# Splitting the first two mixers' projections and output products into high and low halves

## What is computed

```
# even mixer: 4 retention heads of 128, 8 stick-breaking heads of 64
h = x @ w_in_even                       # 1024 x 3584
y = concat(silu(rg) * norm(retention(rotary(rq), rotary(rk), rv)),
           stick_breaking(sq, sk, sv))
x = layer_norm(ALPHA * x + y @ w_out_even); x = layer_norm(ALPHA * x + conv_ffn(x))
# odd mixer: 8 differential heads of 2 x 64
q, k, v = split(x @ w_in_odd)           # 1024 x 3072
p = softmax(q k^T / 8 + rel_bias)       # two per head, causal
o = (p[0] - lam * p[1]) @ v;  o = rms(o) * sub_g * (1 - lam_init)
x = layer_norm(ALPHA * x + o @ w_out_odd); x = layer_norm(ALPHA * x + conv_ffn(x))
```

## Time and profile before

| | us |
|---|---|
| median of 3 runs | 2521.33 (2520.19 to 2523.63) |
| the profiled execution | 2520.85 |
| its span, first to last instruction | 2519.2 |
| PE busy in the span | 2223.6 (88%) |
| DVE, ACT, POOL busy | 1326.6, 1000.7, 332.1 |
| TensorE clock granted, mean | 0.934 |

### The profile page before, as it was taken

The page is one execution under the profiler, slowest core; times in us unless marked ns, Lnnn a source line. Parts: engine busy times, 40 slices in busy tenths (PEclk is TensorE's granted clock), DMA queues, the critical chain, the costliest instruction groups (busy, mean ns, idle before and its releaser), DMA issues. The chain is left out here.

```text
span 2519.2 us, 27351 instructions
## 1 busy us (share of the span) xinstructions
PE 2223.6 (88%) x9734; PEld 1639.5 (65%) x9734; DVE 1326.6 (53%) x1786; ACT 1000.7 (40%) x1100; POOL 332.1 (13%) x299
## 2 busy tenths in 40 slices
PE   8989988999997889799999986757792999999994
PEld 4446647888885555448888875646452788777773
DVE  1221025555442333426554445997613898888885
ACT  1114323343321333303343323123311787777783
POOL 1000000000000000000000001757201122222221
PEclk9989999999998999899999997878885999999997
DMA  9011205743225210204332223211014999999995
GB/s 279 26 43 67 67 17 192 242 117 100 101 67 146 57 50 18 67 0 130 89 108 84 101 67 73 67 50 34 17 37 150 346 398 399 399 398 400 397 399 212
DMA packets 283158, 378.58 MB, mean 150 GB/s; under 512 B 13385, under 2 KB 181501, under 8 KB 282937
## 3 DMA queue, kind: packets, MB, share of 16 engines
q1 hardware_dynamic: 266216, 317.24, 37.6%
q0 software_dynamic: 16848, 60.09, 6.4%
HBM read 341.08 MB, written 38.84 MB: 151 GB/s over the span
## 5 line engine op out<-in xcount | busy, mean ns | idle before, releaser
L845 PE MATMUL PS<-XS,split 128*128 128x512 f32 (+1 forms) x2304 | 486.2, 374 | 13.0 <-DVE split L157 9.9
L845 PEld LDWEIGHTS PS<-XS,split 128*128 128x128 f32 x2304 | 410.4, 191 | 88.6 <-issue 10.3
L157 DVE TENSOR_TENSOR moe_split<-moe_raw,moe_split 128x2048 fp32r<-128x2048 f32 x174 | 397.8, 2288 | 87.1 <-ACT moe_split L152 86.8
L152 ACT CAST moe_split<-moe_raw 128x2048 fp32r<-128x2048 f32 x174 | 332.6, 1913 | 72.2 <-DMA moe_raw<-in_expert_w_gate 37.8
L2285 PE MATMUL PS<-moe_split,moe_x 128*128 128x512 f32 x1392 | 347.7, 400 | 8.6 <-DVE moe_split L157 4.8
L2285 PEld LDWEIGHTS PS<-moe_split,moe_x 128*128 128x128 f32 x1392 | 258.6, 190 | 72.6 <-DVE moe_x L157 13.9
L157 DVE TENSOR_TENSOR split<-ring,split 128x2048 fp32r<-128x2048 f32 x68 | 155.7, 2292 | 220.0 <-ACT split L152 220.0
L878 PE MATMUL PS<-split,XS 128*128 128x512 f32 x960 | 218.4, 389 | 0.3 <-DVE XS L157 0.3
L152 ACT CAST split<-ring 128x2048 fp32r<-128x2048 f32 x78 | 148.1, 1903 | 154.5 <-PE PS L878 110.8
L878 PEld LDWEIGHTS PS<-split,XS 128*128 128x128 f32 x960 | 180.1, 188 | 38.4 <-issue 1.1
L614 PE MATMUL PS<-ring,W 128*128 128x512 f32 x384 | 170.3, 603 | 2.9 <-issue 0.8
(11 more groups left out here) (338 smaller groups left out, 2496.3 us busy)
## 6 DMA issues: line engine op xcount, KB each, us to landing
moe_raw<-in_expert_w_gate SPq DMA_DIRECT2D x58, 1024.0 KB, 13.8
moe_raw<-in_expert_w_up SPq DMA_DIRECT2D x58, 1024.0 KB, 13.9
moe_raw<-in_expert_w_down SPq DMA_DIRECT2D x58, 1024.0 KB, 13.4
ring<-in_w_up SPq DMA_DIRECT2D x88, 512.0 KB, 5.2
ring<-in_w_down SPq DMA_DIRECT2D x44, 512.0 KB, 4.3
expert_rows<-rows POOLq DMA_DIRECT2D x4, 4096.0 KB, 30.4
expert_rows<-W POOLq DMA_DIRECT2D x29, 512.0 KB, 7.0
ring<-in_w_in_even SPq DMA_DIRECT2D x56, 256.0 KB, 5.2
```

Source lines behind the costliest of these rows:

```text
L152: act.copy(hi, raw).then_inc(sem, 1)
L157: return dve.tensor_tensor(lo, raw, hi.bitcast(F32), ALU.subtract)
L845: mm = pe.matmul(PS[:, b + q, rows], w[:, c, q, :], x_half(k, high)[:, c, rows], start=(c == 0 and m == 0), stop=(c == KC - 1 and m == 2))
```

## The change

All projections of both mixers and both output products become three products of halves. The weights come in "pieces" of 128x2048, 18 in the even block and 16 in the odd block, through the 4 raw slots and the 3 slots of `split`. q and k of a head (or pair) are one piece; v comes for two heads (or pairs) at once, in matmuls of 256 columns, and one turn of PE makes half of the tokens.

```diff
+def piece_high(k, act, n):
+    slab = k.pieces[n]
+    slab_ready(k, act, slab)
+    if n >= SPLIT:
+        act.wait_ge(k.piece_used, n - SPLIT + 1)
+    split_high(k, act, k.ring[:, slab[0], :], k.split[:, piece_slot(k, n), 1, :], k.piece_highs)
+def piece_low(k, dve, n):
+    slab = k.pieces[n]
+    dve.wait_ge(k.piece_highs, n + 1)
+    ...
+    split_low(dve, ...).then_inc(k.freed[slab[0]], 1)
```

`entry` copies high halves on ACT and adds low halves on DVE, and splits pieces 0 and 1 behind them. In retention, ACT and DVE split two more pieces per head:

```diff
@@ retention_stage, scalar
         for h in range(H):
             for part in range(2):
                 ...
                 act.copy([qT, kT][part], PS[:, part, :]).then_inc(qk_out, 1)
+            piece_high(k, act, 2 * h + 4)
...
             if h + 1 < H:
                 keep(h + 1, 2)
                 keep(h + 1, 3)
+                piece_high(k, act, 2 * h + 5)
             act.wait_ge(y_turned, h + 1)
             act.copy(YT[:, h, :], PS[:, 2, :]).then_inc(y_out, 1)
```

The stick stage makes four turns ahead (q, k and both halves of v of two pairs), then 3, 3, 2 and 0 turns within the pairs, each of which waits for the keep of the turn two before it; DVE halves the first seven chunks of y while the last pair is on its way (`halve_y`). The output stage multiplies piece 0 for all four tiles and then pieces 1 to 3 tile by tile, and `tail.early` now stands one tile earlier on ACT:

```diff
+        for t in range(NT):
+            mm = product(0, t)
+        mm.then_inc(k.piece_used, 1)
+        for t in range(NT):
+            for i in range(1, 4):
+                ...
+                mm = product(i, t)
...
+            if t == NT - 2 and tail.early:
+                tail.early.scalar(act)
```

The tail of the first feed-forward now writes halves too, and during it ACT and POOL split the first odd piece. In the differential stage POOL makes all low halves but the last, and loads the bias, which has two buffers now:

```diff
@@ diff_stage
+    def lows(pool, h):
+        for u in after[h]:
+            if u in follows and follows[u] < len(k.pieces) - 1:
+                piece_low(k, pool, follows[u])
     def gpsimd(pool):
         ...
+        for h in range(HD):
+            if h > 1:
+                pool.wait_ge(biased, 4 * (h - 2) + 4)
+            src = ...
+            pool.dma_start(bias[:, h % 2, :], src).then_inc(bias_in, 16)
+            if h > 1:
+                pool.wait_ge(bias_in, 16 * (h + 1))
+            if h == 1:
+                for n in (1, 2, 3, 4):
+                    piece_low(k, pool, n)
+                lows(pool, 0)
+            if h > 0:
+                lows(pool, h)
+        pool.wait_ge(early_high, 1)
+        split_low(pool, YT[:, 0:EARLY, :], ...).then_inc(early_low, 1)     # EARLY = 6
@@ scalar, keep(u), behind the copy
+            if u in follows and follows[u] < len(k.pieces) - 1:
+                piece_high(k, act, follows[u])
@@ vector
-        dve.wait_ge(bias_in, 16 * HD)
         for h in range(HD):
+            dve.wait_ge(bias_in, 16 * max(h + 1, 2))
             if h > 0:
                 mix(h - 1, 3)
```

More of the change, by code:

```diff
@@ L419, in sync @@
         w = A["w_in_even"][0]
[L420 to L423, removed]
-    def tensor(pe):
[L426 to L437, removed]
+        for n in (QK0, V01, QK1, V23, QK2, QK3):
+            if n in (V01, V23):
+                load_slab(k, sp, k.pieces[n], [columns(w, 3072 + 256 * (n == V23), 256)])
+            else:
+                p = (QK0, QK1, QK2, QK3).index(n)
+                load_slab(k, sp, k.pieces[n], [columns(w, 2048 + p * P + 512 * part, P) for part in range(2)])
@@ L438, in project @@
+    def tensor(pe):
+        def project(u):
+            n, what, which = turns[u]
+            if u >= 2:
+                pe.wait_ge(kept, u - 1)
+            elif u == 0:
                 pe.wait_ge(k.ret_kept, 16)
                 pe.wait_ge(k.ret_rotated, 16)
[L440 to L448, removed]
@@ L449, in project @@
-            if part == 2:
-                for t in range(NT):
-                    for c in range(KC):
[L452 to L457, removed]
+            bank = 6 + u % 2
@@ L482, in tensor @@
                 mm.then_inc(scored, 1)
-            if p < 3:
-                for part in range(3):
-                    project(p + 1, part)
+            for u in after[p]:
+                project(u)
             for hh in range(2):
@@ L647, in norm_tail @@
     k.rows_used = (normed, NT)
-    split = name in ("even", "odd", "ffn1")
+    split = name != "out2"
     xt_high = k.sem(name + "_xt_high")
@@ L651, in norm_tail @@
     st = k.stat
-    pair = (lambda t: 2 * (t % 2)) if name != "ffn0" and name != "ffn1" else (lambda t: 2 * t)
+    pair = (lambda t: 2 * t) if split else (lambda t: 2 * (t % 2))
+    turn_pair = (0, 0, 4, 6) if name in ("even", "odd") else (0, 2, 4, 6) if split else (4, 4, 4, 4)
     src = (lambda t: X[:, t, :]) if mode == "ln" else (lambda t: hrow[:, t % nh, :])
@@ L816, in early_scalar @@
         act.sem_inc(split_used, AHEAD)
-        high_w(act, 0, 0)
-        act.wait_ge(mixer_tail.product, NT)
-        high_w(act, 1, 0)
+        for i in range(2):
+            act.wait_ge(k.piece_used, len(k.pieces) - 2 + i)
+            high_w(act, i, 0)
     def early_vector(dve):
@@ L850, in tensor @@
     def tensor(pe):
+        pe.drain().then_inc(k.piece_used, 1)
         for turn in range(2):
@@ L1118, in project @@
                 for c in range(KC):
-                    mm = pe.matmul(PS[:, bank, :], view[c // 4][:, c % 4, part, :], k.XT[:, c, :],
-                                   start=(c == 0), stop=(c == KC - 1))
-            else:
-                for t in range(NT):
+                    for m, (w, high) in enumerate(((wh, 1), (wh, 0), (wl, 1))):
+                        mm = pe.matmul(PS[:, bank, :], w[:, c, part], x_half(k, high)[:, c, :],
+                                       start=(c == 0 and m == 0), stop=(c == KC - 1 and m == 2))
+            else:
+                half = turns[u][3]
+                for t in (2 * half, 2 * half + 1):
@@ L1183, in tensor @@
                 value(h - 1, 3)
-            more[0]()
+            project(after[h][0])
             turn_w(h, 0)
@@ L1189, in tensor @@
             score(h, 3)
-            more[1]()
+            project(after[h][1])
             if h > 0:
@@ L1194, in tensor @@
             turn_w(h, 2)
-            more[2]()
+            project(after[h][2])
             value(h, 2)
@@ L1246, in scalar @@
             rows(h, 1)
-            more[0]()
+            keep(after[h][0])
             leave_w(h, 0)
@@ L1253, in scalar @@
             rows(h, 3)
-            more[1]()
+            keep(after[h][1])
             if h > 0:
@@ L1257, in scalar @@
             leave_w(h, 2)
-            more[2]()
+            keep(after[h][2])
+            if h == EARLY:
+                act.wait_ge(projected, len(turns))
+                act.drain()
+                act.copy(x_half(k, 1)[:, 0:EARLY, :], YT[:, 0:EARLY, :]).then_inc(early_high, 1)
         leave_w(HD - 1, 3)
```

424 lines of the change are left out of this document (288 added, 136 removed).

## The result

The changed kernel takes 2525.73 us (median of 20 runs, 2523.12 to 2533.96), the one before 2521.98 us (20 runs) beside it: a ratio of 1.0017, 95% interval 1.0010 to 1.0024. The forecast was 2510. So the change is slower by 0.17%, less than the 0.2% that the prediction called no change. The profiled execution took 2523.86 us (span 2522.3), against 2520.85 before.

What follows compares the result with a forecast made beforehand. PE, busy 88% of the span, was taken as the bound; 7 - 12.6 - 15.5 - 18.8 - 18.6 + 3.5 + 44.4 = -10.6 from 2520.85 gave 2510 us, range 2483 to 2537.

Steps and rivals of the forecast that it cites:

- Price of the products: All changed stages: 0.227 us per fp32r product of 512 columns, 0.114 per 256; PE relieved of 107.7 us together.
- Clock: Slow clock after PE's new pauses: 3 us in retention, +8 in the differential stage, about 2 after each 11 us stop.
- Waits: New PE waits: retention 8.3 us for ACT's cast; differential stage +8, +15.6, +38.1 and, in head 7, +13.9.
- the bias: Differential stage: transfer issued behind POOL's low halves, +11.3 in heads 2, 4, 6, +2.1 in 3, 5; together +38.1.
- rival 2: Differential stage: bias tile lands late beside SP's 1 MB, at 7.8 us; 2533, slower; chance 0.25.
- POOL's hold: Differential stage: POOL's low half stops DVE, +4.6 us each in heads 1, 3, 5 and +1.8 in head 0; +15.6.
- rival 1: Differential stage: POOL's low halves don't hold DVE, so 15.6 and 7.2 us go; 2487; chance 0.17.
- The k cast: Differential stage: ACT casts 1.90 us before leave_y in heads 0, 2, 4, 6; +2.0 each, +8.
- The entry: Kernel start: DVE's low halves and the first piece's cast and low half delay PE, +7 us.
- both output products: Even and odd output stages with the feed-forward's first tokens: -18.8 and -18.6 us; the even one from 79.0 to 60.2.
- the tail: End of the first feed-forward: two pairs of low halves in DVE's chain and 0.9 us behind the last turn, +3.5.
- Rival 3: Some twenty new PE pauses add slow clock, or a semaphore hop is missing; gain and loss cancel at 2521; chance 0.10.

Runs made afterwards that it cites:

- the first experiment: The changed kernel with POOL issuing head h+1's bias transfer ahead of the low halves of head h in the differential stage: 2467.67 us, ratio 0.9784.
- the quarters: The changed kernel with the bias issued ahead of the low halves and POOL's weight-piece low halves as four 512-column instructions, differential stage: 2475.08 us, ratio 0.9822.

## Why the prediction was wrong

The direction of every stage was right, the sum was not: -10.6 us against +3.0 in the profiled executions (2520.85 and 2523.86). The 13.6 us by terms (rounded), with -0.3 from the stages that came within about 1 us and -2.0 behind them:

- **Price of the products, 12.7 us.** I took 0.227 us from the feed-forward's 960 products and 0.114 from 44. In the differential stage a turn of 24 takes 5.73 us, not 5.45, and a v half 6.00. 16 turns from 7.03 to 5.73 give 20.8 instead of 25.3, v from 58.5 to 11.74 + 6 x 6.00 = 47.7 gives 10.8 instead of 14.9. In retention 16 products of 13.90 became 48 of 11.15, eight times: 22.0 instead of 23.9. In the stick stage the eight turns give 11.3 instead of 12.6 and v 5.5 instead of 7.4, and 2.2 of these 3.2 us show in the length of the stage. A price per product from long rows leaves out what each short row pays once: 24 products take 5.73 us and 48 take 11.15, which is 0.226 each and 0.3 a row. For 256 columns 48 take 6.00 and 96 take 11.74, 0.120 each and 0.26 a row, so there the price itself was low too. The row to take was the turn.
- **Clock, 12.1 us.** Forecast 3 in retention and 8 in the differential stage. Retention's busy time fell by 13.4 us, the products alone by 22.0: 8.6. The differential stage's fell by 17.1 instead of 31.6: 14.5. These two are what is left when the products are taken out, but the granted clock fell with them, from 0.97 to 0.91 and from 0.93 to 0.81, and the first experiment gave 13.1 back with the same instructions. The prediction took the price of a short stop from one turn of 8.20 us; behind the same wait of 2.21 us head 1 of the kernel before has 7.13 and heads 2 to 6 have 7.71 to 8.12. The direct test, a pause in the kernel before, gave 10.4 us for 27 us of waiting, where I had 2 per long stop. And stops of 2.6 us, for which I had 1, put scores of 2.42 at 3.8 to 4.6.
- **Waits, -8.8 us.** In retention 6.6 instead of 8.3, in the differential stage 69.5 instead of 76.6. There, by the forecast's own steps: the bias in heads 2, 4 and 6, 10.9, 11.9 and 9.8 (forecast 11.3 each); in heads 3 and 5, 3.2 and 1.6 (2.1 each); head 7, 11.7 (13.9). The bias landed 4.3, 5.2, 5.3, 5.2, 3.2 and 3.3 us after its issue, 4.4 in the mean (4.0); SP's 1 MB ran beside it as rival 2 said, but its 7.8 us did not come. POOL's hold cost 4.2 us in heads 1, 3 and 5 (4.6), so rival 1 fell. The instruction held there is not one of mix, as I had said, but the scaling behind the bias sums (L1476). The k cast cost 1.35 in three heads, not 2.0 in four: head 0 has no leave_y.
- The entry (+6.0), both output products (-18.1, -18.2) and the tail (+3.1) came within 1 us. For the odd product the prediction shows no working: the 60.2 us of the even one would have made -20.5 of 80.7.

So the steps that failed are two terms of the sum. The price of a product was taken at 0.227 and 0.114 us where the turns measured 0.239 and 0.125. The clock was taken at 3 and 8 us where 8.6 and 14.5 came out. Together they are 24.8 us short, covered in part by waits counted too high. A difference of 10.6 between terms of over 90 us each way can't carry a sign at that accuracy. Rival 3, at a chance of 0.10, named one of the two, the clock, and no price. That its 2521 is nearly the total is luck: the waits counted too high stood against the price.

## What to carry to other kernels

Take the price of a product from a row as long as the one that will run, and put beside each new wait of PE its share for the clock: here 0.3 to 0.4 of it for stops of 7 to 12 us, half and more for stops of 2 us. That is an average, and no closer than some 10 us for a whole stage: the quarters raised busy time by 14.8 us while the waits fell. When an engine issues transfers in program order with its work, ask of each transfer when its buffer came free, and issue it there; here that one line was worth 58 us. And look in the kernel before at the waits that repeat in every head: the cheapest 30 us of this study were there.

## What was not expected

- The same sequence with the same waits ran at a granted clock of 1.00 or 0.85 (29.5 and 33.9 us a head). The mean clock of the whole kernel is steady from run to run, 0.918 in all five runs of the one kernel and 0.922 to 0.925 in those of the other, so this is no scatter between runs. But it is no fixed trait of a kernel's heads either. Heads 1 and 2 of the kernel before, the same instructions and a wait of 2.21 us in both:
```profile
842.14:874.51 32.37, 28.85 (x147) 18.24 (x146) 12.15 (x53) 11.18 (x27) 0.00 (x0) 1.00 0.16 45
874.51:908.49 33.98, 30.46 (x148) 18.75 (x147) 12.15 (x53) 11.18 (x27) 0.00 (x0) 0.95 0.03 5
```
Two other kernels lost 3 us in stretches with unchanged instructions. What decides besides the wait no run here shows. The Trainium skill, "TensorE: Matmul & The Clock Gate" (What's actually happening), says that the number of slow products at a start varies from run to run; here the traces agree only in that the same work can meet either clock.
- POOL does not hold every DVE instruction between SBUF tiles, as the earlier trace rows had let me think. In head 0 of the changed kernel:
```profile
785.19 4.60 POOL L152 TENSOR_TENSOR split<-ring,split 128x2048 fp32r<-128x2048 f32 x1 [7.39 <-ACT split L147]
...
787.34 0.17 DVE L1483 RECIPROCAL cols<-cols 128x2 f32<-128x2 f32 x1 [2.12 <-ACT W L1414]
787.59 0.21 DVE L1487 TENSOR_SCALAR cols<-cols,lam 128x1 f32<-128x1 f32 x1
787.72 2.15 DVE L1488 TENSOR_SCALAR W<-W,cols 128x128 f32<-128x128 f32 x1
```
The reciprocal of 128 x 2 elements and the scaling of 128 x 1 take their usual 0.17 and 0.21 us in the middle of POOL's low half; the scaling of 128 x 128 behind them, 0.28 us alone, stands to POOL's end at 789.8. In the first experiment's head 7:
```profile
998.05 4.53 POOL L152 TENSOR_TENSOR split<-ring,split 128x2048 fp32r<-128x2048 f32 x1 [15.98 <-ACT split L147]
...
1001.63 0.28 DVE L1475 CUSTOM_DVE_ANT_0 W<-PS,W 128x128 f32<-128x128 f32 x1
...
1002.04 0.57 DVE L1478 TENSOR_SCALAR cols<-cols 128x2 f32<-128x2 f32 x1
```
The sum over PSUM and one SBUF tile takes its usual 0.28 us; the scaling of 128 x 2 elements, 0.17 us alone, waits for POOL's end at 1002.58. So the amount of work does not decide, and the memory alone does not either, since the reciprocal and this scaling have the same tile and shape. The kind of instruction counts; the full rule no run here shows.
